# Attention stage: probabilities scaled before plain transposes, and two heads per instruction

## What is computed

```python
s_loc = jnp.einsum('bjqhd,bijlhd->bhjqil', qb, k_blk).astype(jnp.float32)
bias = jnp.moveaxis(bias_cols[:, rel_r], 1, 3)
s_loc = jnp.where(col_valid[:, :, None, :], s_loc + bias, NEG_INF)
s_ctx = jnp.einsum('bjqhd,bkhd->bhjqk', qb, k_c).astype(jnp.float32)
s = jnp.concatenate([s_loc.reshape(B, H, n_cb, NA_QBLOCK_W, n_loc), s_ctx], axis=-1)
p = jax.nn.softmax(s, axis=-1).astype(v_g.dtype)
...
o = (jnp.einsum('bhjqil,bijlhd->bjqhd', p_loc, v_blk)
     + jnp.einsum('bhjqk,bkhd->bjqhd', p_ctx, v_c))
```

## Time and profile before

| | us |
|---|---|
| median of the runs (1920.11, 1921.41, 1926.1) | 1921.41 |
| the profiled execution | 1922.82 |
| its span, from the first to the last instruction | 1921.0 |
| TensorE busy in it | 1833.4 |
| VectorE busy | 1220.0 |
| ScalarE busy | 728.3 |
| the attention stage, from its first scores to the first matmul of `na_out` | 68.0 |

### The profile page before, as it was taken

How to read it: one execution, slowest core, us unless ns; L and a number is a source line. 1 busy time by engine, 2 the same in 40 slices (tenths; PEclk the granted TensorE clock), 3 DMA queues, 4 the chain that set the end, 5 groups by cost and what they waited for, 6 DMA issues and landing times.

```text
span 1921.0 us, 25350 instructions
## 1 busy us (share of the span) xinstructions
PE 1833.4 (95%) x9680; PEld 1539.9 (80%) x9680; DVE 1220.0 (64%) x2020; ACT 728.3 (38%) x1003; POOL 62.6 (3%) x39
## 2 busy tenths in 40 slices
PE   6899999999889799999999999999999999989998
PEld 2688888877788587888888878888888797789998
DVE  4677677778999854777577357766333434755554
ACT  2522122336766833322132252312322434654343
POOL 0000000020000001000000100000002000010001
PEclk7999999999989998999999999999999999989999
DMA  7444545331110122554464235444223241034553
GB/s 298 154 175 157 188 183 209 120 113 66 45 45 28 39 72 104 186 202 148 148 235 146 94 129 192 172 153 178 95 77 113 107 176 55 2 111 174 179 183 120
DMA packets 39860, 257.81 MB, mean 134 GB/s; under 512 B 4688, under 2 KB 5840, under 8 KB 14832
## 3 DMA queue, kind: packets, MB, share of 16 engines
q1 hardware_dynamic: 39792, 256.92, 37.1%
HBM read 255.85 MB, written 1.05 MB: 134 GB/s over the span
## 4 chain that ended last, share of the span: by engine, by line
PE 84%; DVE 10%; ACT 3%; issue 2%; DMA 1%; SPq 0%; DVEq 0%; ACTq 0%
PE ps_all L1574 26%; PE ps_all L1578 25%; PE ps_all L1575 25%; DVE w_lo L924 2%; PE ps_all L1964 2%; PE bank L1622 1%; DMA start_scale<-in_w_scale 1%; PE bank L1977 1%; PE bank L2000 1%; ACT w_hi L538 1%; DVE cp L432 1%; DVE stat L1307 1%; PE bank L1789 1%; DVE wb L1238 0%; DVE normed L1294 0%
## 5 line engine op out<-in xcount | busy, mean ns | idle before, releaser
L1574 PE MATMUL ps_all<-a_hi,w_lo 128*128 128x512 f32 (+1 forms) x1800 | 663.4, 369 | 21.5 <-ACT a_hi L648 14.0
L1578 PE MATMUL ps_all<-a_lo,w_hi 128*128 128x512 f32 (+1 forms) x1800 | 657.4, 365 | 0.2 <-DVE a_lo L1063 0.2
L1575 PE MATMUL ps_all<-a_hi,w_hi 128*128 128x512 f32 (+1 forms) x1800 | 657.2, 365 | 0.0
L924 DVE TENSOR_TENSOR w_lo<-w_raw,w_hi 128x2048 fp32r<-128x2048 f32 (+3 forms) x184 | 376.5, 2046 | 162.1 <-ACT w_hi L538 160.9
L538 ACT ACTIVATE w_hi<-w_raw 128x2048 fp32r<-128x2048 f32 (+3 forms) x183 | 313.5, 1713 | 338.4 <-PE ps_all L1578 331.0
L1574 PEld LDWEIGHTS ps_all<-a_hi,w_lo 128*128 128x128 f32 x1800 | 345.5, 192 | 79.7 <-issue 16.2
L1578 PEld LDWEIGHTS ps_all<-a_lo,w_hi 128*128 128x128 f32 x1800 | 345.2, 192 | 56.8 <-DVE a_lo L1063 4.1
L1575 PEld LDWEIGHTS ps_all<-a_hi,w_hi 128*128 128x128 f32 x1800 | 345.8, 192 | 52.1 <-issue 0.2
L936 DVE SCALAR_TENSOR_TENSOR mod_junk<-mod_raw,cond 128x1024 bf16<-128x1024 f32 x256 | 302.7, 1220 | 5.4 <-ACT cond L566 2.7
L1574 PE MATMUL ps_all<-g_hi,w_lo 128*128 128x512 f32 (+1 forms) x704 | 258.4, 367 | 1.0 <-DVE w_lo L924 1.0
L1578 PE MATMUL ps_all<-g_lo,w_hi 128*128 128x512 f32 (+1 forms) x704 | 258.3, 367 | 0.0
(11 more groups left out here) (236 smaller groups left out, 1512.0 us busy)
## 6 DMA issues: line engine op xcount, KB each, us to landing
w_raw<-in_tiles SPq DMA_DIRECT2D x118, 1024.0 KB, 4.8
mod_raw<-in_w_mod SPq DMA_DIRECT2D x64, 1024.0 KB, 4.8
w_raw<-in_tiles SPq DMA_DIRECT2D x32, 768.0 KB, 4.1
w_raw<-in_tiles SPq DMA_DIRECT2D x32, 640.0 KB, 3.7
start_raw<-in_w_mod SPq DMA_DIRECT2D x4, 1024.0 KB, 16.1
start_scale<-in_w_scale SPq DMA_DIRECT2D x4, 1024.0 KB, 20.2
bias<-in_na_bias SPq DMA_DIRECT2D x2, 1536.0 KB, 8.9
cond<-in_cond SPq DMA_DIRECT2D x2, 1024.0 KB, 6.0
```

The source lines that it names most:

```text
L924: nc.vector.tensor_tensor(w_lo[:, slot, 0:size], w_raw[:, slot, 0:size], w_hi[:, slot, 0:size].bitcast(F32), ALU.subtract).then_inc(lo_rea ...
L1574: pe.matmul(dst, w[1], x[0], start=start, stop=False)
L1575: pe.matmul(dst, w[0], x[0], start=False, stop=False)
L1578: return pe.matmul(dst, w[0], x[1], start=False, stop=stop_)
```

## The change

- A pair's probabilities are multiplied by the reciprocals in place, in `prob`. VectorE does it with a tensor_scalar of 128x512 elements per head (`scale_probs`), but for head 1 of odd pairs, which ScalarE scales (`scaled_by_act`). The diagonal and its tile are gone.
- `turn_probs` uses transposes against the constant identity, through the helper `turn`. It waits for the whole pair to be scaled (`scaled`, and `scaled_act` for head 1 of odd pairs), and from the second pair on for the copy of the pair before as a whole.
- Bias sum, maximum and reciprocal are one instruction for both heads of a pair. For this the four single banks become one tensor `banks`.
- `exps` waits once for the pair's maxima; `copy_turned` is one instruction of 128x1024.
- Ahead of the loop VectorE makes both maxima first, and then scales both pairs.

```diff
--- before.py
+++ after.py
@@ -230,7 +230,8 @@
 
         ps_all = ctx.enter_context(nc.psum_tensor("ps_all", [P, 4, 512], F32))
         ps = [ps_all[:, 2 * n:2 * n + 2] for n in range(2)]
-        bank = [ctx.enter_context(nc.psum_tensor(f"bank{n}", [P, 512], F32)) for n in range(4)]
+        banks = ctx.enter_context(nc.psum_tensor("banks", [P, 4, 512], F32))
+        bank = [banks[:, n] for n in range(4)]
         ps_mod, ps_sum = bank[2], bank[3]
         glu_to = [[ps[0][:, 0, :], ps[0][:, 1, :]], [bank[2][:], bank[0][:]]]
 
@@ -296,7 +297,6 @@
             k_t = sbuf("k_t", [P, KT, T], F32, na)
             v_tok = sbuf("v_tok", [P, 4, D], F32, na)
             prob_t = sbuf("prob_t", [P, 4, T], F32, na)
-            diag = sbuf("diag", [P, 4, P], F32, na)
             negmax = sbuf("negmax", [P, UNITS], F32, na)
             rowsum = sbuf("rowsum", [P, UNITS], F32, na)
             recip = sbuf("recip", [P, UNITS], F32, na)
@@ -331,7 +331,7 @@
             "loads", "gam_in", "qk", "swapped", "rope", "gam", "exp1", "slope", "least", "cross", "exp2", "mask", "s", "p", "o",
             "osq", "kept", "gated", "sum", "std", "rstd", "spread", "mixed", "cast", "mix", "y_split", "ymix")}
         na_sem = {n: sem("na_" + n) for n in (
-            "bias", "masked", "s", "added", "max", "exp", "recip", "diag", "turned", "copied", "o",
+            "bias", "masked", "s", "added", "max", "exp", "recip", "scaled", "scaled_act", "turned", "copied", "o",
             "hi", "mix")}
         out_stored = sem("out_stored")
 
@@ -404,7 +404,11 @@
                 return None
             return first + per * (it - begin) + slot if begin else first + per * it + slot
 
-        score_bank = [ps_all[:, 0, :], ps_all[:, 1, :], bank[2][:, :], bank[3][:, :]]
+        score_bank = [ps_all[:, 0:2, :], banks[:, 2:4, :]]
+
+        def scaled_by_act(j, n):
+
+            return j % 2 == 1 and n == 1
 
         PAIRS = UNITS // 2
 
@@ -855,22 +859,28 @@
                 def exps(j):
 
                     _, _, at = pair_of(j)
+                    act.wait_ge(N["max"], j + 1)
+                    if j >= 2:
+                        act.wait_ge(N["turned"], 2 * j - 2)
                     for n in range(2):
                         u = 2 * j + n
-                        act.wait_ge(N["max"], u + 1)
-                        if j >= 2:
-                            act.wait_ge(N["turned"], u - 3)
-                        nc.scalar.activation(prob[at + n], score_bank[at + n], ACT.Exp, bias=negmax[:, u:u + 1],
+                        nc.scalar.activation(prob[at + n], score_bank[j % 2][:, n], ACT.Exp, bias=negmax[:, u:u + 1],
                                              accum_out=rowsum[:, u:u + 1]).then_inc(N["exp"], 1)
+
+                def scale_probs(j):
+
+                    _, _, at = pair_of(j)
+                    act.wait_ge(N["recip"], j + 1)
+                    nc.scalar.activation(prob[at + 1], prob[at + 1], ACT.Copy,
+                                         scale=recip[:, 2 * j + 1:2 * j + 2]).then_inc(N["scaled_act"], 1)
 
                 def copy_turned(j):
 
                     _, _, at = pair_of(j)
                     if j >= 2:
                         act.wait_ge(N["o"], 2 * j - 2)
-                    for n in range(2):
-                        act.wait_ge(N["turned"], 2 * j + n + 1)
-                        nc.scalar.activation(prob_t[:, at + n, :], ps[1][:, n, :], ACT.Copy).then_inc(N["copied"], 1)
+                    act.wait_ge(N["turned"], 2 * j + 2)
+                    nc.scalar.activation(prob_t[:, at:at + 2, :], ps[1][:, :, :], ACT.Copy).then_inc(N["copied"], 1)
 
                 def high(tile):
 
@@ -882,10 +892,13 @@
 
                 exps(0)
                 exps(1)
+                scale_probs(1)
                 for j in range(PAIRS):
                     copy_turned(j)
                     if j + 2 < PAIRS:
                         exps(j + 2)
+                        if scaled_by_act(j + 2, 1):
+                            scale_probs(j + 2)
                     if j >= 2 and j % 2 == 0:
                         high(j // 2 - 1)
                 high(PAIRS // 2 - 1)
@@ -1450,28 +1463,25 @@
                 def maxima(j):
 
                     tile, s, at = pair_of(j)
+                    dve.wait_ge(N["s"], 2 * j + 2)
+                    local = score_bank[j % 2][:, :, NCTX:T]
+                    nc.vector.tensor_tensor(local, local, bias[:, 2 * tile:2 * tile + 2, 2 - 2 * s:6 - 2 * s, :].rearrange("p h r c -> p h (r c)"),
+                                            ALU.add).then_inc(N["added"], 1)
+                    dve.wait_ge(N["added"], j + 1)
+                    nc.vector.tensor_reduce(negmax[:, 2 * j:2 * j + 2], score_bank[j % 2], AX.X, ALU.max,
+                                            negate=True).then_inc(N["max"], 1)
+
+                def scale_probs(j):
+
+                    _, _, at = pair_of(j)
+                    dve.wait_ge(N["exp"], 2 * j + 2)
+                    nc.vector.reciprocal(recip[:, 2 * j:2 * j + 2], rowsum[:, 2 * j:2 * j + 2]).then_inc(N["recip"], 1)
+                    dve.wait_ge(N["recip"], j + 1)
                     for n in range(2):
-                        u = 2 * j + n
-                        dve.wait_ge(N["s"], u + 1)
-                        local = score_bank[at + n][:, NCTX:T]
-                        nc.vector.tensor_tensor(local, local, bias[:, 2 * tile + n, 2 - 2 * s:6 - 2 * s, :].rearrange("p r c -> p (r c)"),
-                                                ALU.add).then_inc(N["added"], 1)
-                        dve.wait_ge(N["added"], u + 1)
-                        nc.vector.tensor_reduce(negmax[:, u:u + 1], score_bank[at + n], AX.X, ALU.max,
-                                                negate=True).then_inc(N["max"], 1)
-
-                def diagonals(j):
-
-                    _, _, at = pair_of(j)
-                    for n in range(2):
-                        u = 2 * j + n
-                        dve.wait_ge(N["exp"], u + 1)
-                        nc.vector.reciprocal(recip[:, u:u + 1], rowsum[:, u:u + 1]).then_inc(N["recip"], 1)
-                        dve.wait_ge(N["recip"], u + 1)
-                        if j >= 2:
-                            dve.wait_ge(N["turned"], u - 3)
-                        nc.vector.tensor_scalar(diag[:, at + n, :], const[:, C_IDENT:C_IDENT + P], recip[:, u:u + 1], None,
-                                                ALU.mult).then_inc(N["diag"], 1)
+                        if not scaled_by_act(j, n):
+                            ins = nc.vector.tensor_scalar(prob[at + n], prob[at + n], recip[:, 2 * j + n:2 * j + n + 1], None,
+                                                          ALU.mult)
+                    ins.then_inc(N["scaled"], 1)
 
                 def low(tile):
 
@@ -1483,13 +1493,14 @@
                         ALU.subtract).then_inc(N["mix"], 1)
 
                 dve.wait_ge(N["masked"], 4)
-                for j in range(2):
-                    maxima(j)
-                    diagonals(j)
+                maxima(0)
+                maxima(1)
+                scale_probs(0)
+                scale_probs(1)
                 for j in range(PAIRS):
                     if j + 2 < PAIRS:
                         maxima(j + 2)
-                        diagonals(j + 2)
+                        scale_probs(j + 2)
                     if j >= 2 and j % 2 == 0:
                         low(j // 2 - 1)
                 low(PAIRS // 2 - 1)
@@ -1949,26 +1960,26 @@
                         pe.wait_ge(N["exp"], 2 * j - 2)
                     for n in range(2):
                         rows = slice(64 * n, 64 * n + 64)
-                        pe.matmul(score_bank[at + n], q_t[rows, tile, s * P:(s + 1) * P], k_t[rows, tile, :],
+                        pe.matmul(score_bank[j % 2][:, n], q_t[rows, tile, s * P:(s + 1) * P], k_t[rows, tile, :],
                                   start=True, stop=True).then_inc(N["s"], 1)
 
                 def turn_probs(j):
 
                     _, _, at = pair_of(j)
+                    pe.wait_ge(N["scaled"], j + 1)
+                    if j:
+                        pe.wait_ge(N["copied"], j)
                     for n in range(2):
-                        u = 2 * j + n
-                        pe.wait_ge(N["diag"], u + 1)
-                        if j:
-                            pe.wait_ge(N["copied"], u - 1)
+                        if scaled_by_act(j, n):
+                            pe.wait_ge(N["scaled_act"], j // 2 + 1)
                         for t in range(4):
-                            mm = pe.matmul(ps[1][:, n, t * P:(t + 1) * P], prob[at + n][:, t * P:(t + 1) * P], diag[:, at + n, :],
-                                           start=True, stop=True)
+                            mm = turn(ps[1][:, n, t * P:(t + 1) * P], prob[at + n][:, t * P:(t + 1) * P])
                         mm.then_inc(N["turned"], 1)
 
```

(2 more changed lines are left out.)

## The result

The changed kernel takes 1931.87 us (median of seven runs) against 1921.05 before: 10.8 us longer, a ratio of 1.0055 with a 95% interval of 1.0039 to 1.0071. The profiled execution took 1932.33 us, its span 1930.3.

What follows compares the result with a forecast made beforehand. TensorE was taken to bound the kernel, busy 95% of the span; after the change VectorE and ScalarE would bound the attention stage. Loop 9.4, start 0.4, end 0.4 and clock 3.5 gave +13.7 on 1921.4: 1935 us, range 1927 to 1940.

Steps and rivals of the forecast that it cites:

- The loop: Steady attention pairs: VectorE's chain through ScalarE takes 9.47 us per two pairs against 8.12, adding 9.4 us over fourteen pairs.
- the scaling: VectorE's in-place multiply of 128x512 probabilities by reciprocals: 0.68 us, issued every 0.60, at L1060's rate.
- the low part: The a_lo instruction on VectorE in every second pair, holding its queue 0.33 us.
- ScalarE's scaling: Head 1 of odd pairs, scaled on ScalarE after the reciprocal: 0.63 us, by a copy of the same shape.
- two elements per ns: Rival on VectorE's scaling: issued every 0.34 us instead of 0.60, total 1929, or 1925.7 at full clock; chance 0.12.
- Start and end: The attention stage's first scores to pair 2's sum, and last pair's sum to output projection: +0.4 us each at full clock.
- The clock's part: TensorE's clock falls after long gaps: +3.5 us, 2.0 at the stage's start and 1 to 2 at its end.
- The long gaps: TensorE idle about 4.2 us at the stage's start, 3.4 before the last turning, 1.1 and 2.4 in the loop.
- Full clock throughout: Rival: TensorE keeps full clock in the attention stage, so only +10.2 us, total 1931.5; chance 0.18.
- Cheap paired instructions: Rival in VectorE's loop: paired sum 0.47, maximum 0.69, scalings at the cast's rate, 7.11 per two pairs, total 1914; chance 0.03.
- dear transposes: Rival in TensorE's turning: transposes cost the old 1.98 us per pair, only start and end pay, +15.9, total 1937; chance 0.05.
- Low clock for most of the stage: Rival: every TensorE gap of 2.4 us brings a low stretch, +15 to +20 us, total 1936 to 1942; chance 0.07.

Runs made afterwards that it cites:

- perhead: The changed kernel with sum, maximum, reciprocal and scaling again per head, each waiting for its own exponential only; stage 67.0 us against 78.3, whole 0.9989 of the kernel before.
- ahead: The changed kernel reordered: scores three pairs ahead, sum and maximum of pair j + 3 before reciprocal and scaling of j + 2; stage 57.1 us, 0.9953 of the kernel before.
- fill: The changed kernel with unread matmuls put into TensorE's gaps, at start, end and before odd pairs' turnings; stage 74.7 us against 78.3, run once.
- before_paired: The kernel before, with only bias sum and maximum merged into one instruction each for both heads; stage 69.6 us against 68.0, whole 1.0018 of the kernel before.

## Why the prediction was right

**The mechanism.** The chain leaves TensorE and closes over VectorE and ScalarE. It is shown by the chain after, and by its undoing: perhead takes out the wait and the loss goes, ahead fills it and turns the loss into a gain. The forecast's condition, that nothing but the reciprocal stands in VectorE's queue behind the maximum, is what the order ahead takes away; perhead leaves the queue's order and lets each head's step start on its own.

**The loop.** Sum 0.73, maximum 1.22, 1.52 us from maximum to reciprocal, 0.20 to the scaling, 0.33 for the low part: each was met within 0.02 us (chain after: 1667.20 + 1.22 to 1669.94 is 1.52). The step that failed is the scaling: 0.68 us, issued every 0.60, was forecast; 0.487, issued every 0.40, was measured. Three per two pairs make 0.60 us, and 9.47 - 0.60 = 8.87 is the loop's 8.86. So 9.4 us forecast for the loop stand against 58.4 - 52.1 = 6.3 measured between the sums of pairs 2 and 15, 0.7 of it by the clock. Two of the named signs failed by this, the period of 9.4 to 9.5 us and the scaling of 0.68. ScalarE's scaling was mis-sized the other way, 0.72 us for a forecast of 0.63, which cost the loop nothing: the next exponentials wait 0.76 us for their maximum behind it.

The reason is how were read. L1060, 412 ns for 256 elements, was split into 0.15 us of fixed cost and one element per ns. It reads two columns. With 0.06 us for each it is 0.16 + 0.12 + 0.13, at two elements per ns. One row with one size can't tell rate from fixed cost. A second was there, the diagonal at L1473 with 128 elements and one column, 0.29 us: 0.16 + 0.06 + 0.07. The Trainium skill ("VectorE: DVE Perf Modes", The perf-mode tier table) gives fp32 tensor_scalar in SBUF two elements a cycle, and the measured rate agrees: 512 elements in 0.26 us beside the fixed 0.16. I had set that rule against a row, and the row said something else. The rival "two elements per ns" was thus right in its rate, and its 1929 was 3 us too low, as the forecast's 1935 was 3 too high: it had 0.43 us per scaling and took the excess of the loop for 4.0. The time alone doesn't decide between the two; the measured 0.487 us lies far nearer to the rival.

**Start and end.** +0.4 and +2.0 by the clock were forecast at the start, +1.8 in all was measured; at the end +0.4 and 1.5, measured +2.1. The clock's part, 3.5 forecast, is 3.6 by fill, but not where I put all of it: 1.6 at the start, 1.2 at the end, 0.7 in the loop, where I had said that half clock is affordable. It isn't quite. The scores of an odd pair come 0.3 us late when turning and scores both run slow. The long gaps themselves were forecast well: 4.2 us at the start, 3.4 at the end and 2.4 in the loop, for 4.12, 3.38 and 2.3 measured. The short one of the loop is 0.25 us and not 1.1.

**The sum.** 13.7 forecast, 10.3 in the stage and 10.8 in the runs. Without the clock 10.2 were forecast, and fill shows 6.7: 5.6 in the loop for 9.4, 0.2 at the start for 0.4, 0.9 at the end for 0.4. Between the sums of pairs 2 and 15 VectorE scales 20 times, each 0.20 us cheaper than forecast: 4.0 us, which is the whole miss of the loop and more than that of the sum.

**The other rivals.** Full clock throughout named 1931.5, almost the measured time, and is refuted all the same: by luck its scaling, 4.0 us too dear, stands in for the 3.6 us of clock that it leaves out. Cheap paired instructions are refuted by 693 and 1224 ns for sum and maximum, dear transposes by 1.02 us for eight at full clock. That is more than the 0.9 forecast, but nobody waits for it in the loop. Low clock for most of the stage didn't occur: its mean over the stage is 0.91.

## What to carry to other kernels

- Merging two instructions of one engine saves their fixed cost, here about 0.16 us each (two sums of 0.43 us became one of 0.69). If another engine starts on the first half's result, it also ends an overlap, here 0.4 us per pair for the maxima and as much again for the scalings. Before merging, look at who starts between the two.
- A gain on the bounding engine counts only down to the next chain. Work out the serial loop through the other engines, waits included, and not their busy shares: both were busy for three quarters of the stage or less, and the expectation of before_paired works the loop through them out at 4.0 us, against TensorE's 4.06, as soon as the pairs are merged.
- If that loop is the bound, first put the next piece's independent work into its wait. Here this was the difference between +10.3 and -12.9 us in the stage, with the same instructions but for one scaling in four.

## What the runs showed of the hardware that I had not expected

- A tensor_scalar of VectorE on 128x512 fp32 in SBUF takes 424 ns with a constant, 484 with one column of scalars and 544 with two: 60 ns per column, beside two elements per ns.
- fp32 transposes of 128x128 follow each other every 0.13 us at full clock (1.02 us for eight), ordinary fp32 matmuls of the same size every 0.25 (1.98 us for eight).
- In the loop of the changed kernel gaps of TensorE of 2.12 and 2.33 us were followed by a low clock and two others, of 2.31 and 2.32 us, by full clock, within one execution: the length of the gap alone doesn't tell it. With filler matmuls in those gaps TensorE kept 1.00 through the whole stage. What decides it stays open. Two of the four, eight transposes each:

```profile
1649.77 1.07 PE L1581 MATMUL ps_all<-const,normed 128*128 128x128 f32 x8 [2.31 <-ACT prob_t L883]
1658.64 1.68 PE L1581 MATMUL ps_all<-const,normed 128*128 128x128 f32 x8 [2.33 <-ACT prob_t L883]
```
